# One factor for two stacked RMS norms: squares and split beside the product before, three projection tiles on the unnormed pair

## The reference

```python
def swa_layer(x, ...):                       # last layer of the first block
    ...
    return x + (o * jax.nn.silu(gate)) @ w_out

def first_block(...):
    ...
    return rms_norm(h, final_norm)[:, N_META:]         # y * gain, y = xf * rsqrt(mean(xf^2) + 1e-5)

def second_block(x, ...):
    for l in range(DEPTH_2):
        u = _rms_norm(x, norm_mix_pre[l])              # the same with 1e-6
        mix = hybrid_mixer(u, w_in[l], ...)            # proj = u @ w_in, 2048 x 12580, first of all
        x = x + _rms_norm(mix, norm_mix_post[l])
        ...
```

## Time and profile before

| | |
|---|---|
| time, median of 3 runs | 2810.07 us (2806.48 to 2812.39) |
| time of the profiled execution | 2812.88 us |
| its span, from the first to the last instruction | 2811.1 us |
| granted TensorE clock, mean share of full speed | 0.972 |
| busy PE / PE weight load / DVE / ACT / POOL | 2669.8 / 2578.7 / 1041.4 / 1188.2 / 1896.4 us |
| mean memory traffic | 151 GB/s |

### The profile page before, as it was taken

One profiled execution on the slowest core, in us unless ns is written; L12 is line 12 of the kernel. 1 busy time (PEld: TensorE's weight loads), 2 busy tenths in 40 slices (PEclk: granted clock), 3 DMA queues, 4 the chain that ended last, 5 costly groups with the idle time before them and its releaser, 6 DMA issues.

```text
span 2811.1 us, 57641 instructions
## 1 busy us (share of the span) xinstructions
PE 2669.8 (95%) x23922; PEld 2578.7 (92%) x23922; DVE 1041.4 (37%) x1362; ACT 1188.2 (42%) x1377; POOL 1896.4 (67%) x786
## 2 busy tenths in 40 slices
PE   6999999989999979989999999999889999999996
PEld 5999999989998979989898989999889999999996
DVE  4434444245664031125464646423242131220312
ACT  3444444455664334443434343333344343343432
POOL 3766776775666838556464646587658888788884
PEclk9999999999999989899999999999999999999998
DMA  4545554554454535444343434366546666566663
GB/s 168 157 144 150 151 157 143 149 166 120 137 147 132 179 118 174 128 126 136 99 148 101 147 97 145 114 188 196 149 120 187 187 182 191 174 189 185 179 191 106
DMA packets 120026, 425.68 MB, mean 151 GB/s; under 512 B 12672, under 2 KB 18944, under 8 KB 119552
## 3 DMA queue, kind: packets, MB, share of 16 engines
q1 hardware_dynamic: 115104, 416.54, 49.7%
q10 hardware_dynamic: 4704, 5.77, 0.6%
HBM read 418.07 MB, written 4.19 MB: 150 GB/s over the span
## 4 chain that ended last, share of the span: by engine, by line
PE 90%; DVE 6%; ACT 3%; issue 1%; DMA 0%; ACTq 0%; SPq 0%; DVEq 0%
PE ps L216 19%; PE ps L218 19%; PE ps L225 19%; PE ps L270 16%; PE ps L1618 4%; PE ps L261 2%; PE ps L257 2%; PE ps L256 2%; PE ps L961 1%; ACT wh L197 1%; DVE og L374 1%; DVE hl L302 1%; DVE hl L2082 1%; PE ps L647 1%; DVE xT L2090 1%
## 5 line engine op out<-in xcount | busy, mean ns | idle before, releaser
L2292 POOL TENSOR_TENSOR wl<-raw,wh 128x1024 fp32r<-128x1024 f32 x782 | 1896.2, 2446 | 880.5 <-ACT wh L197 879.3
L197 ACT ACTIVATE wh<-raw 128x2048 fp32r<-128x2048 f32 x391 | 748.0, 1913 | 720.1 <-PE ps L225 442.3
L216 PE MATMUL ps<-hh,wh 128*128 128x256 f32 (+1 forms) x3248 | 813.1, 288 | 44.3 <-DVE hl L302 35.2
L218 PE MATMUL ps<-hl,wh 128*128 128x256 f32 (+1 forms) x3248 | 808.1, 287 | 0.0
L216 PEld LDWEIGHTS ps<-hh,wh 128*128 128x128 f32 x3248 | 622.7, 192 | 52.9 <-issue 29.7
L218 PEld LDWEIGHTS ps<-hl,wh 128*128 128x128 f32 x3248 | 623.9, 192 | 0.0
L225 PE MATMUL ps<-hh,wl 128*128 128x256 f32 (+1 forms) x3248 | 425.7, 284 | 0.0
L225 PEld LDWEIGHTS ps<-hh,wl 128*128 128x128 f32 x3248 | 406.7, 189 | 0.0
L216 PE MATMUL ps<-gh,wh 128*128 128x256 f32 x1264 | 301.4, 280 | 0.0
L218 PE MATMUL ps<-gl,wh 128*128 128x256 f32 x1264 | 301.0, 280 | 0.0
L216 PEld LDWEIGHTS ps<-gh,wh 128*128 128x128 f32 x1264 | 237.7, 188 | 0.4 <-issue 0.2
(11 more groups left out here) (345 smaller groups left out, 3022.0 us busy)
## 6 DMA issues: line engine op xcount, KB each, us to landing
raw<-weights SPq DMA_DIRECT2D x782, 512.0 KB, 3.6
xT<-tokens SPq DMA_DIRECT2D x1, 2176.0 KB, 8.7
spill<-xT ACTq DMA_DIRECT2D x1, 2048.0 KB, 7.5
xT<-spill ACTq DMA_DIRECT2D x1, 2048.0 KB, 10.2
out<-xT SPq DMA_DIRECT2D x1, 2048.0 KB, 7.5
C<-consts SPq DMA_DIRECT2D x1, 2000.0 KB, 11.9
arena<-lora ACTq DMA_DIRECT2D x4, 384.0 KB, 3.2
P<-params SPq DMA_DIRECT2D x1, 125.0 KB, 12.9
```

Source lines behind the costliest of these rows:

```text
L197: nc.scalar.activation(wh[:, m % 2, :, :].rearrange("p a b -> p (a b)"), raw[:, 2 * (m % 2):2 * (m % 2) + 2, :, :].rearrange("p a b c -> p ...
L216: nc.tensor.matmul(acc[0:m, 0:n], wh[:, slot, kt, 0:m], rh[:, kt, 0:n], start=(kt == kts[0]), stop=False)
L218: nc.tensor.matmul(acc[0:m, 0:n], wh[:, slot, kt, 0:m], rl[:, kt, 0:n], start=False, stop=False)
L2292: nc.gpsimd.tensor_tensor(wl[:, s // 2, h, :], raw[:, s, :, :], wh[:, s // 2, h, :].bitcast(F32), ALU.subtract)\
```

## The change

Both norms are computed from sums over `h` alone. With m1 = mean(h^2) and m2 = mean((h g1)^2), the first factor is r1 = 1/sqrt(m1 + 1e-5), and the mean square that the second norm sees is r1^2 m2, so the product of both factors is r = 1/sqrt(m2 + 1e-6 (m1 + 1e-5)). `u` is h g1 g2 r. In the changed kernel:

- `TwoNorms` takes the place of both `Norm`s. Per tile of `b_out`, ACT squares the new block twice (with and without g1), writes `og = xT * g1 g2` and its high part `uh`; DVE adds the two squares side by side (128x512) and writes the rest `ul`. One DVE product of the gains stands ahead of that.
- `zz` tiles 0 to 2 read the pair (`uh`, `ul`), which lacks the factor r. PE sums the squares within tile 0 (`pe_sum`, after its 32 high-weight matmuls), and spreads r1 and r over the partitions within tile 1 (`pe_all`). DVE lands these three tiles times r (`land`).
- From tile 3 on the pair (`hh`, `hl`) is read as before. DVE writes og * r into PSUM by quarters (`norm`), ACT copies it to `hh` (`act_pair`), DVE writes `hl` (`rest`).
- The 16 blocks `xT * g1 * r1` come last on DVE, and the transfer to `spill` is issued after ACT has landed tile 8. The table for the root is loaded at the end of attention b.

```diff
+        class TwoNorms:
+            def __init__(self, name, gains, n, ready, temps):
...
+                self.running = ps[:, 5, :]
+                self.means = ps[:, 4, 0:8].rearrange("p (a b) -> p a b", b=2)[:, :, 0]
+            def act(self, eng, kt):
+                A, V, n = self.A, self.V, self.n
+                x = xT[:, kt, 0:n]
+                sq = self.sq[:, kt % 2, :] if kt else self.running
+                eng.wait_ge(self.ready[0].sem, self.ready[1][kt])
+                eng.wait_ge(V.sem, V.at(f"l{kt - 2}") if kt >= 2 else V.at("gain"))
+                nc.scalar.activation(sq[:, 0:n], x, ACT.Square)
+                nc.scalar.activation(sq[:, n:2 * n], x, ACT.Square, scale=p(self.gains[0], kt))\
+                    .then_inc(A.sem, A.step(f"q{kt}"))
+                nc.scalar.activation(og[:, kt, 0:n], x, ACT.Copy, scale=self.both[:, kt:kt + 1])\
+                    .then_inc(A.sem, A.step(f"y{kt}"))
+                eng.wait_ge(A.sem, A.at(f"y{kt}"))
+                nc.scalar.activation(uh[:, kt, 0:n], og[:, kt, 0:n], ACT.Copy)\
+                    .then_inc(A.sem, A.step(f"h{kt}"))
+            def dve(self, eng, kt):
+                A, V, n = self.A, self.V, self.n
+                if kt:
...
+                    nc.vector.tensor_tensor(self.sum if kt == KT - 1 else self.running, self.running,
+                                            self.sq[:, kt % 2, :], ALU.add)\
+                        .then_inc(V.sem, V.step(f"s{kt}"))
+                eng.wait_ge(A.sem, A.at(f"h{kt}"))
+                nc.vector.tensor_tensor(ul[:, kt, 0:n], og[:, kt, 0:n], uh[:, kt, 0:n].bitcast(F32), ALU.subtract)\
+                    .then_inc(V.sem, V.step(f"l{kt}"))
+            def pe_sum(self, eng):
+                eng.wait_ge(self.V.sem, self.V.at(f"s{KT - 1}"))
+                for k in range(4):
+                    ins = mm(ps[:, 4, 2 * k:2 * k + 2], self.sum[:, 128 * k:128 * k + 128], eps[:, 4:6])
+                ins.then_inc(self.T.sem, self.T.step("sum"))
...
+            def act_root(self, eng):
+                eng.wait_ge(self.V.sem, self.V.at("v2"))
+                nc.scalar.activation(self.col, self.col, ACT.Sqrt)\
+                    .then_inc(self.A.sem, self.A.step("root"))
+            def pe_all(self, eng):
+                eng.wait_ge(self.V.sem, self.V.at("col"))
+                for k in range(4):
+                    ins = mm(self.running[:, 128 * k:128 * k + 128], self.col[:, k:k + 1].to_broadcast([128, 128]),
+                             c("ident"))
+                ins.then_inc(self.T.sem, self.T.step("all"))
+            def normed(self, k):
+                return ps[:, 2 * (k % 2):2 * (k % 2) + 2, :].rearrange("p a (b n) -> p (a b) n", b=2)
+            def act_pair(self, eng, k):
+                eng.wait_ge(self.V.sem, self.V.at(f"m{k}"))
+                nc.scalar.activation(hh[:, 4 * k:4 * k + 4, 0:self.n], self.normed(k), ACT.Copy)\
+                    .then_inc(self.A.sem, self.A.step(f"n{k}"))
+            def dve_pair(self, eng):
...
+                r1, r = self.running[:, 0:n], self.running[:, n:2 * n]
+                def land(t):
+                    eng.wait_ge(tile_done, done("zz", t))
+                    nc.vector.tensor_tensor(fz["z"][:, t, :], ps[:, 6 + t % 2, 0:n], self.rs, ALU.mult)\
+                        .then_inc(V.sem, V.step(f"z{t}"))
+                def norm(k):
+                    if k >= 2:
+                        eng.wait_ge(V.sem, V.at(f"l_{k - 2}"))
+                    nc.vector.tensor_tensor(self.normed(k), og[:, 4 * k:4 * k + 4, 0:n],
+                                            r.unsqueeze(1).to_broadcast([128, 4, n]), ALU.mult)\
+                        .then_inc(V.sem, V.step(f"m{k}"))
+                def rest(k):
...
+                    nc.vector.tensor_tensor(hl[:, f, 0:n], self.normed(k), hh[:, f, 0:n].bitcast(F32), ALU.subtract)\
+                        .then_inc(V.sem, V.step(f"l_{k}"))
...
+                nc.vector.tensor_copy(self.rs, r)\
+                    .then_inc(V.sem, V.step("rs"))
...
+                for kt in range(KT):
+                    nc.vector.scalar_tensor_tensor(out=xT[:, kt, 0:n], in0=xT[:, kt, 0:n], scalar=p(self.gains[0], kt),
+                                                   in1=r1, op0=ALU.mult, op1=ALU.mult)\
+                        .then_inc(V.sem, V.step(f"x{kt}"))
...
+                    if t == 3:
+                        opening(pe, "zz", acc, hh, hl, SEQ, Quarters(two.V, "l_"), t).then_inc(tile_done, 1)
+                    elif t < 3:
+                        for k in range(6):
+                            if t == 0 and k in (0, 3):
+                                pe.wait_ge(two.V.sem, two.V.at("l11" if k == 0 else "l15"))
+                            if t == 0 and k == 4:
+                                two.pe_sum(pe)
+                            if t == 1 and k == 1:
+                                two.pe_all(pe)
+                            ins = part(pe, "zz", t, k, acc, uh, ul, SEQ)
+                        ins.then_inc(tile_done, 1)
...
-            act.wait_ge(norm_mix.V.sem, norm_mix.V.at(norm_mix.last))
+            two.act_root(act)
             act.dma_start(fr["lw"], lora[:, 0:2, :]).then_inc(lora_in, 16)
-            land(range(0, 13))
+            land(range(0, 1))
+            two.act_pair(act, 0)
+            two.act_pair(act, 1)
+            land(range(1, 2))
+            two.act_pair(act, 2)
+            two.act_pair(act, 3)
+            land(range(2, 9))
+            act.wait_ge(two.V.sem, two.V.at(f"x{KT - 1}"))
+            act.dma_start(spill, xT[:, :, 0:SEQ]).then_inc(x_spilled, 16)
+            land(range(9, 13))
```

More of the change, by code:

```diff
@@ L139, in build @@
         st = sb("st", [128, 64])
-        eps = sb("eps", [128, 4])
+        eps = sb("eps", [128, 6])
         ARENA = nc.sbuf_bytes_remaining // 4 - 8
@@ L147, in build @@
         gh, gl = sb("gh", [128, KT, SEQ], F32R), sb("gl", [128, KT, SEQ], F32R)
+        with nc.sbuf_tensor("uh", [128, KT, SEQ], F32R) as uh, nc.sbuf_tensor("ul", [128, KT, SEQ], F32R) as ul:
+            pass
         PAIR = 2 * KT * SEQ
@@ L229, in build, with opening @@
         ALL = range(KT)
-        def opening(pe, phase_name, acc, rh, rl, n, split):
-            q = FIRST[phase_name]
+        def opening(pe, phase_name, acc, rh, rl, n, split, t=0):
+            q = FIRST[phase_name] + t
             pe.wait_ge(hi_done, q + 1)
@@ L476, in build, with __init__ @@
+        class Quarters:
+            size = 4
+            class V:
+                pass
+            def __init__(self, steps, name):
+                self.V = Quarters.V()
+                self.V.sem = steps.sem
+                self.V.at = lambda l: steps.at(f"{name}{l[1:]}")
         class Product:
@@ L1065, in attn_b_act @@
             split_bo.quarter_act(act, SB["v"], SB["v"].at("o", STEPS_B - 1), 3)
+            nc.scalar.activation(st[:, ROOT:ROOT + 1], eps[:, 3:4], ACT.Sqrt)
         def attn_b_dve(dve):
@@ L1141, in attn_b_dve @@
             split_bo.quarter_dve(dve, 3)
-        b_out = Product("b_out", "b_out", (gh, gl), SEQ, xT, add=True, split=split_bo)
-        norm_fin = Norm("norm_fin", xT, SEQ, 0, [("fin", xT, None)], written=b_out.written(), after="zz")
-        split_mix = Split("split_mix", og, (hh, hl), SEQ)
-        norm_mix = Norm("norm_mix", xT, SEQ, 1, [("mix_pre", og, split_mix)],
-                        written=(norm_fin.V, [norm_fin.V.at(f"o0_{4 * k + 3}") for k in range(4)]))
+        b_out = Product("b_out", "b_out", (gh, gl), SEQ, xT, add=True, split=split_bo, after="zz")
+        two = TwoNorms("two", ("fin", "mix_pre"), SEQ, b_out.blocks(),
+                       carve([("pairs", 2 * PAIR), ("sq", 2, 2 * SEQ), ("sum", 2 * SEQ), ("gain", KT), ("col", 4), ("rs", SEQ)]))
         NCH = SEQ // CHUNK
-        SZ = phase("zz", a=" ".join(f"z{t}" for t in range(33)))["a"]
+        SZ = phase("zz", a=" ".join(f"z{t}" for t in range(3, 33)))["a"]
         SLZ = phase("land_z", v="om l0 l1 l2 l3 l4 l5")["v"]
@@ L1189, in dense @@
                         pe.wait_ge(SLZ.sem, SLZ.at(f"l{t - 29}"))
+                    elif t >= 5:
+                        pe.wait_ge(SZ.sem, SZ.at(f"z{t - 2}"))
                     elif t >= 2:
-                        pe.wait_ge(SZ.sem, SZ.at(f"z{t - 2}"))
-                    tile(pe, "zz", t, 0, 0, [(ps[:, 6 + t % 2, :], hh, hl, ALL)], SEQ, m=SMALL.get(t, 128),
-                         ready=first(0, t, split_mix)).then_inc(tile_done, 1)
+                        pe.wait_ge(two.V.sem, two.V.at(f"z{t - 2}"))
+                    acc = ps[:, 6 + t % 2, :]
+                    if t == 3:
[10 more added lines that the diff above has]
+                        ins.then_inc(tile_done, 1)
+                    else:
+                        tile(pe, "zz", t, 0, 0, [(acc, hh, hl, ALL)], SEQ, m=SMALL.get(t, 128)).then_inc(tile_done, 1)
             def turn_v(zv, step):
@@ L1282, in land @@
                     round_weights(act, "zz", t + 2)
```

(18 more changed lines are left out.)

50 lines of the change are left out of this document (46 added, 4 removed).

## The result

The changed kernel takes **2785.36 us** (median of 4 runs, 2780.14 to 2789.09), the kernel before beside it 2811.23 us (4 runs, 2806.48 to 2814.39). The ratio is 0.9905, 95% interval 0.989 to 0.992. The gain is real, but it is 25.9 us in place of 39.8, and 2785.4 lies above the range of 2766 to 2782. The profiled execution took 2785.98 us, with a span of 2784.1.

The account below looks back on a forecast made before the run. PE was busy only 38.77 of 59.00 us between `b_out` and 1032.50, waiting for both norms. Three tiles 17.07 + 0.10 + 0.76 + 1.13 = 19.06 us replace 58.89, so 2810.07 - 39.8 = 2770.3 us; range 2766 to 2782.

Parts of the forecast that it names:

- The stretch to tile 3: From the end of `b_out` to the start of `zz` tile 3: 19.06 us in place of 58.89, 39.83 less.
- The waits inside it: PE's waits in `zz` tiles 0 to 3: 0.1 us for the last block, 0 for the factor and the pair.
- Added matmuls: On PE, summing the squares within `zz` tile 0, 0.76 us, and spreading the factors within tile 1, 1.13 us.
- the sum: Whole kernel: 39.8 us off the profiled execution and off the median, giving 2770.3 us, ratio 0.986.
- the supply: Weight loads beside the transfer to `spill` after tile 8: 0, bound 2.8 us; as rival 1 to 5 us, chance 0.10.
- Lower clock: PE without its pause gets the lower clock, up to 6.4 us more per tile; 2816 us, chance 0.02.
- The other rivals: PE waits around `zz` tiles 0 to 3: pair late, 0.12; last block, sum or factor not covered, 2780 us, 0.08.
- the late pair: Before `zz` tile 3, eight DVE instructions contend with POOL at 3.0 us each; 2781 to 2786 us, chance 0.12.

Follow-up runs that it names:

- -96: The changed kernel as it is, its mlp loop starting 96 PE instructions earlier than in the kernel before; 2785.36 us, ratio 0.9905.
- +160: The kernel before with 160 PE instructions that only wait, ahead of the two norms behind mix_out; 2833.54 us, ratio 1.0062.

## Why the prediction was wrong

- **The stretch to tile 3** was right: 18.84 us against 19.06, and the loop written out in both kernels gives the forecast ratio of 0.986 within 0.001, with some luck of the clock in it (above).
- **The waits inside it.** `ul` 15 ended at 976.11 (976.2 foretold), the factor was spread at 982.0 (982.0), the last rest of the pair stood at 993.9 (994.2), the eight instructions took 1.22 us each. The Trainium skill ("SBUF — State Buffer", section Who interferes with whom) says that a VectorE instruction with two SBUF inputs contends with a GpSimd one that reads SBUF, and one with at most one SBUF input does not. The traces agree: 1.22 us with an operand in PSUM, 1.21 to 3.42 us with both in SBUF.
- **Added matmuls:** from start to start as in the earlier trace rows, 0.81 us for the sum (977.23 to 978.04) and 0.80 for the spreading (980.95 to 981.75), for 0.76 and 1.13.
- **The step that failed is the sum**: "The profiled execution becomes 2811.1 - 39.8". It took all behind tile 3 as unchanged, and its only entry for that was the supply. The change shifts PE's program by 96 instructions, and the cost of the two jumps back of the mlp loop, 5.6 us before, became 16.2. This 10.6 us (3.3 + 7.4 by the leads) is a term that the sum did not have. The profile of before had it in sight, a wait of 1.69 us with releaser "issue" at 2600.57, and I read past it. The Trainium skill ("Runtime: NRT & Kernel Launch", section Instruction fetch mechanics) says that instructions come in blocks of 256, prefetched in sequence, and that a jump out of the window stalls for a fetch. The loop written out, with no stall, the like cost at -96 and +160, and the packets of 16.4 KB, fewer with the loop written out, agree with that; that the cost swings between 3.4 and 16.2 us with the place is what the runs add.
- **The supply** was given 0, with a bound of 2.8: it cost 1.3 in the profiled run and nothing in most others. The term held only by its cover: it had been put at 0 because the loads in the earlier trace rows show no lengthening, yet ACT waited up to 7.91 us for a load here, and the transfer took 14.1 us.
- **Lower clock:** in `zz` it stayed at 1.00, so the rival fell. It went below that behind the stalls, 0.87 in the stretch from 2381.60.
- **The other rivals** fell too: no wait of PE in tiles 0 to 3. The measured time lies in the range that the late pair would have given (2781 to 2786), but by another cause.
- Together: 40.1 - 1.3 - 1.2 - 10.7 = 26.9 us, against 27.0 between the spans.

The best version measured is the changed kernel with the loop written out, 2768.37 and 2771.18 us.

## What to carry to other kernels

When PE is busy nearly all the time, look for its waits with releaser "issue" and ask whether a loop of the engine jumps back there. An edit anywhere ahead of it moves its place and can give or take time that has nothing to do with the edit, here up to 13 us (3.4 to 16.3), so time the edit with the loop written out as well. Padding of instructions that only wait is a way to test this, but only where the engine stands idle; on PE's path 96 of them cost some 11 us.

## What the runs showed of the hardware

A run of small fp32 matmuls in the mixer (line 272; 270 in the kernel before) starts at the full clock. In twelve of the fourteen traces the clock falls to the lower level 4 to 10 us into it, and a pair of records of 128x128 takes 0.63 us in place of 0.39; in the two of the changed kernel with nothing but its loop written out it does not fall. The changed kernel's windows view, then that of the one with the loop written out, over the same work:

```profile
1135.00:1153.00 18.00, 18.00 (x66) 13.51 (x66) 0.11 (x1) 2.29 (x3) 4.99 (x3) 0.61 0.36 111
```

```profile
1133.00:1144.50 11.50, 11.50 (x66) 8.72 (x66) 0.00 (x0) 2.29 (x3) 5.23 (x3) 1.00 0.55 176
```

That is 6.5 us, with the same instructions, and 7.7 over the whole run by the roundings. The medians hold it in a share that no trace shows; the profiled runs with the short form are also among the shortest of their kernel (2762.99 and 2764.03 us, of 2760.77 to 2778.81). What tips it is open.
